# Expert lookups of a two-layer step: six units in one run, the part between the layers beside them, tile by tile

## The reference, cut to what matters

```python
ue = expert_u[idx]          # rows of 1024 floats, 128 for each token
ve = expert_v[idx]
act = jax.nn.gelu(jnp.einsum('td,thkd->thk', xb, ue).astype(f32))
coef = (gate * act).astype(xb.dtype)
return jnp.einsum('thk,thkd->td', coef, ve)
```

## Time and profile before

| | us |
|---|---|
| median of 3 runs | 3033.41 (3025.52 to 3058.54) |
| the profiled execution | 3040.26 |
| its span, first to last instruction | 3038.2 |
| VectorE busy | 1603.4 |
| TensorE busy | 1891.8 |
| GpSimd busy | 1523.8 |

### The profile page before, as it was taken

The page is one execution under the profiler, slowest core; times in us unless marked ns, Lnnn a source line. Parts: engine busy times, 40 slices in busy tenths (PEclk is TensorE's granted clock), DMA queues, the critical chain, the costliest instruction groups (busy, mean ns, idle before and its releaser), DMA issues. The chain is left out here.

```text
span 3038.2 us, 22434 instructions
## 1 busy us (share of the span) xinstructions
PE 1891.8 (62%) x7072; PEld 904.2 (30%) x7072; DVE 1603.4 (53%) x3822; ACT 284.2 (9%) x603; POOL 1523.8 (50%) x1480
## 2 busy tenths in 40 slices
PE   7999787890019900597767787790019900398547
PEld 4577564370002200122331356470002200122201
DVE  2488853148886079803734242248886078901731
ACT  2133210010000000000110133110000000000000
POOL 0013441017777777777645000017777777777672
PEclk9999887995559955798889867895559955699779
DMA  4332142248889999999888505238899999999896
GB/s 123 110 114 81 42 117 85 103 171 287 306 319 396 409 342 402 387 409 373 315 320 344 184 31 155 96 132 291 312 332 403 408 319 361 370 408 380 310 371 235
DMA packets 301933, 809.18 MB, mean 266 GB/s; under 512 B 26041, under 2 KB 91401, under 8 KB 301793
## 3 DMA queue, kind: packets, MB, share of 16 engines
q0 software_dynamic: 184320, 671.17, 58.5%
q1 hardware_dynamic: 117502, 136.65, 14.0%
HBM read 795.45 MB, written 12.17 MB: 266 GB/s over the span
## 5 line engine op out<-in xcount | busy, mean ns | idle before, releaser
L1919 POOL DMA_INDIRECT arena<-peer_u,arena x640 | 788.4, 1232 | 854.8 <-DVE arena L1599 563.7
L1620 DVE SCALAR_TENSOR_TENSOR arena<-arena,u 128x1024 f32<-128x1024 f32 x640 | 769.8, 1224 | 122.5 <-DMA arena<-peer_u,arena 105.2
L702 PE MATMUL banks<-arena 128*32 128x512 f32 x2560 | 782.2, 619 | 41.4 <-DMA arena<-peer_v,arena 34.8
L1919 POOL DMA_INDIRECT arena<-peer_v,arena x640 | 621.4, 971 | 251.4 <-issue 144.8
L476 PE MATMUL banks<-cst,arena 128*128 128x128 f32 (+5 forms) x522 | 85.7, 321 | 904.4 <-DVE arena L1635 661.3
L498 PE MATMUL banks<-wring,uT 128*128 128x512 f32 (+3 forms) x864 | 383.8, 601 | 12.1 <-DMA wring<-ssm_w_out 5.2
L702 PEld LDWEIGHTS banks<-arena 128*32 128x32 f32 x2560 | 200.1, 111 | 618.9 <-issue 335.5
L476 PEld LDWEIGHTS banks<-cst,arena 128*128 128x128 f32 (+5 forms) x522 | 68.9, 164 | 930.7 <-DVE arena L1635 664.7
L1662 DVE COPY h<-banks 128x512 f32<-128x512 f32 x8 | 5.5, 692 | 479.1 <-PE banks L709 479.1
L498 PEld LDWEIGHTS banks<-wring,uT 128*128 128x128 f32 (+1 forms) x864 | 150.1, 178 | 238.5 <-issue 233.8
L724 PE MATMUL banks<-uT,wring 128*128 128x320 f32 x512 | 140.7, 437 | 2.4 <-ACT uT L1073 2.4
(11 more groups left out here) (206 smaller groups left out, 1720.0 us busy)
## 6 DMA issues: line engine op xcount, KB each, us to landing
wring<-ssm_w_in SPq DMA_DIRECT2D x24, 1024.0 KB, 7.3
wring<-peer_w_query SPq DMA_DIRECT2D x16, 1024.0 KB, 7.4
wring<-ple_w_gate SPq DMA_DIRECT2D x16, 1024.0 KB, 5.8
wring<-w_q SPq DMA_DIRECT2D x12, 1024.0 KB, 8.6
arena<-peer_u,arena POOLq DMA_INDIRECT x640, 6.2
arena<-peer_v,arena POOLq DMA_INDIRECT x640, 7.2
wring<-ssm_w_out SPq DMA_DIRECT2D x8, 1024.0 KB, 7.3
u<-state_ssm SPq DMA_DIRECT2D x16, 512.0 KB, 6.1
```

The source lines that it names most:

```text
L702: mm = pe.matmul(outs[n][at % C], place(t)[:, at % C, at // C, :], rows_buf[:, k, n * 512:(n + 1) * 512], start=at < C, stop=False, skip_g ...
L1620: dve.scalar_tensor_tensor(rows_buf[:, k, :], rows_buf[:, k, :], 1.0, u[:, t, :], ALU.mult, ALU.mult, accum_out=cols[:, bass.ds(i, 1), k]) ...
L1919: pool.indirect_dma_start(rows_buf[:, k, :], None, tables[which], bass.IndirectOffsetOnAxis(ap=rows, axis=0))\
```

## The change

Seven phases follow each other in all engines' programs. Phase p has the u blocks of unit p and the v blocks of unit p-1, in the order of `phase_blocks`: 6 u, the v but 6, the remaining u, the last 6 v. Beside the blocks run side steps, spread evenly by `due`: the remaining selection of layer 0 in phases 0 and 1, the whole part between the layers with the selection of layer 1 for tile 0, 1 and 2 in phases 2, 3 and 4 (`chain(t)`), the embedding of layer 1 in phases 5 and 6, and after them that of tile 2. `chain(t)` is embedding, `kv`, `wq`, heads, attention of this tile alone (`prompt_attention` or `sample_attention`), `wo`, normalisation and `ask(t)`, the queries and picks of this tile.

All these weights are planned and loaded once per tile: the embeddings, `kv` and `wq` three times where it was twice, `wo` and the second queries three times where it was once. Queries of layer 1 are products of 128 or 64 columns where they had 320. Values are summed in banks 6 and 7, with the two halves of a block on different columns of the array for all tiles; the other jobs share six banks. The caches of the samples lie in the weight ring, singly buffered, so that no weights are loaded meanwhile. Dots are written out block by block instead of a loop. One quad is picked before the first gather; the other seven of tiles 0 and 1 lie beside the dots of tile 0.

```diff
-        def claim(pe, key, hold=False):
-            while turn[0] % NB in held:
...
+        def claim(pe, key):
+            b = turn[0] % ring[0]
...
+        UNITS = ((0, 0), (0, 1), (0, 2), (1, 0), (1, 1), (1, 2))
+        BLOCKS = (128, 128, 64)
+        LEAD = 6
+        def phase_blocks(ph):
+            nu = BLOCKS[UNITS[ph][1]] if ph < 6 else 0
+            nv = BLOCKS[UNITS[ph - 1][1]] if ph > 0 else 0
+            i = j = 0
+            while i < nu or j < nv:
+                if j == nv or (i < nu and (i < LEAD or j >= nv - LEAD)):
+                    yield "u", ph, i
+                    i += 1
+                else:
+                    yield "v", ph - 1, j
+                    j += 1
...
+        SIDE_STEPS = (39, 12, 51, 51, 48, 3, 3)
+        def due(ph, i):
+            upto = lambda k: SIDE_STEPS[ph] * k // PHASE_LEN[ph]
+            return upto(i + 1) - upto(i)
...
+            def sums(t, n, half):
+                if t == 2:
+                    at = 64 * half + COLS * (n % 2)
+                    return sum_banks[0][at:at + COLS, :]
+                at = COLS * ((n + 2 * half) % 4)
+                return sum_banks[half][at:at + COLS, :]
...
+            def beside(ph):
+                if ph == 0:
+                    yield from finish_select(0, 0, 5)
+                    yield from select(0, 1)
+                elif ph == 1:
+                    yield from select(0, 2)
+                elif ph < 5:
+                    yield from chain(ph - 2)
+                else:
+                    yield from embed(1, ph - 5)
...
+            for ph in range(7):
+                side = beside(ph)
+                for i, (kind, n, at) in enumerate(phase_blocks(ph)):
+                    if kind == "v":
+                        combine(n, at)
+                    advance(side, due(ph, i))
+                advance(side)
...
-        cache = arena[:, 15728:15728 + 4 * 3328].rearrange(
-            "p (x w b n) -> p x w b n", x=2, w=2, b=26)
+        cache = wring[:, :, :].rearrange("p s d -> p (s d)")[:, 0:2 * 3328].rearrange("p (w b n) -> p w b n", w=2, b=26)
...
-                with dve.Fori(first, last, 1) as i:
-                    for k in range(PSLOTS):
...
+            def dot(n, at):
+                (l, t), (k, use) = UNITS[n], turn_of["u", n, at]
+                dve.wait_ge(gathered[k].sem, 16 * (use + 1))
...
+            for ph in range(7):
+                for kind, n, at in phase_blocks(ph):
+                    (l, t), (k, use) = UNITS[n], turn_of[kind, n, at]
```

More of the change, by code:

```diff
@@ L715, in ffn, with turn_sub_keys, finish_select @@
[L715 removed]
+            def turn_sub_keys(l):
                 pe.wait_ge(*sk_in.at(l))
                 transposes(("sk", l), [(c * 128, sk_raw[:, c, :]) for c in range(2)])
[L718 to L720 removed]
+            def finish_select(l, t, first=0):
+                for _ in range(first, 5 * (HPT[t] // 2)):
+                    yield
+                turn_indices(l, t)
+                yield
@@ L721, in ffn, with select, ask, query @@
+            def select(l, t):
+                scores(l, t, range(HPT[t] // 2))
+                yield
+                yield from finish_select(l, t)
+            def ask(t):
+                R, cols = ROWS[t], slice(OFF[t], OFF[t] + ROWS[t])
+                def query(n):
+                    w = [weight(pe, (f"query1{t}", n, half), ("q1", t, 4 * n + 3)) for half in range(2)]
                     for j in range(4):
-                        acc = claim(pe, ("q", l, 4 * n + j))
+                        bank = claim(pe, ("q1", t, 4 * n + j))
@@ new lines, in ask @@
+                if t == 0:
+                    turn_sub_keys(1)
+                query(0)
+                yield
+                query(1)
+                if t == 0:
+                    pe.wait_ge(*freed(("sk", 1)))
+                if t < 2:
+                    turned(0)
+                    scores(1, t, [0])
+                yield
+                for q in range(4):
+                    if q < 2:
+                        query(q + 2)
+                    if t < 2 and q < 3:
+                        turned(q + 1)
+                        scores(1, t, [q + 1])
+                    if t == 2 and q == 1:
+                        for n in range(4):
+                            turned(n)
+                        scores(1, 2, range(2))
+                    if t < 2 or q < 2:
+                        for _ in range(5 if t < 2 else 1):
+                            yield
@@ L763, in embed @@
+                yield from finish_select(1, t, 20 if t < 2 else 0)
+            def embed(l, t):
+                R, cols = ROWS[t], slice(OFF[t], OFF[t] + ROWS[t])
+                pe.wait_ge(*prow_in.at((l, t)))
+                transposes(("pT", l, t), [(c * 128, p_rows[0:R, c * 128:(c + 1) * 128]) for c in range(2)])
+                norm_transposes(f"ple{l}", (t,))
+                pe.wait_ge(*freed(("pT", l, t)))
                 yield
                 for n in range(2):
-                    w = weight(pe, (f"pproj{l}{group}", n, 0), (f"pproj{l}", n, tiles[-1]))
@@ L1349, in _ @@
+            for ph in range(7):
+                side = beside(ph)
+                for i, (kind, n, at) in enumerate(phase_blocks(ph)):
+                    if kind == "u" and at + 1 == BLOCKS[UNITS[n][1]]:
+                        tanh_of(n)
+                    advance(side, due(ph, i))
+                advance(side)
+                if ph < 6:
+                    place_coefficients(ph)
+            advance(embed(1, 2))
         @block.vector
@@ new lines, in beside @@
+            def beside(ph):
+                if ph == 0:
+                    yield from finish_select(0, 0, 1)
+                    yield from select(0, 1)
+                elif ph == 1:
+                    yield from select(0, 2)
+                elif ph < 5:
+                    yield from chain(ph - 2)
+                else:
+                    yield from embed(1, ph - 5)
+            for n in range(2):
+                for t in range(3):
+                    add_to_h("out", 0, t, n)
+            norm("ffn0", FFN_SLOT)
@@ new lines, in _ @@
+            s(dve.tensor_copy(u[64:128, 2, :], u[0:64, 2, :]))
+            s(dve.memset(place, 0.0), dve_done, "place_zero")
+            advance(pick_quad(0, 0, 0))
+            for ph in range(7):
+                side = beside(ph)
+                for i, (kind, n, at) in enumerate(phase_blocks(ph)):
+                    if kind == "u":
+                        dot(n, at)
+                        if at + 1 == BLOCKS[UNITS[n][1]]:
+                            gelu(n)
+                    advance(side, due(ph, i))
+                advance(side)
+                if ph > 0:
+                    take_peer(*UNITS[ph - 1])
```

1193 lines of the change are left out of this document (588 added, 605 removed).

## The result

The changed kernel takes 3081.5 us (median of 4 runs, 3074.95 to 3084.61); the kernel before took 3040.55 us in the same comparison. The ratio is 1.0129 with an interval of 1.0067 to 1.0192: slower by 1.3%. The forecast was 2991 us and faster by 1.4%, so the change went the other way. The time lies within the stated range, nearest to rival C (3105 us).

The account below looks back on a forecast made before the run. No engine bounds the whole: DMA bounds value stages, VectorE is 85% busy in dot stages, 378 us lack gathers. Start, seven phases, handovers 18 and tail 46 sum to 2996 of span, so 2991 us; range 2840 to 3110.

Parts of the forecast that it names:

- rival C: Whole kernel: waits stall in-order engines, fronts cost 73 us in each of three tiles, slower at 3105 us; chance 0.22.
- Start, phases 0, 2, 3 and 5: Span before the first gather 663 us, then phases of 272, 387, 403 and 272 us.
- Tile 1's dot run: Phase 3: 140 + 28 + 62 of VectorE, then waits for scores and attention and light steps, 257 us.
- dot run: 140 + 19 + 31 + 20 of waiting + 15: Phase 4: VectorE's work, 20 us waiting for scores, 15 for steps with nothing in them, 225 us.
- the caches as 42 us of bytes: Phase 4's value run: 13.6 MB of cached keys and values at 321 GB/s, within a run of 250 us.
- a DMA share under 0.8 in value runs: Value runs: the sign that would show the slower rival, stalled in-order engines, to be right.
- its queries at the lower clock: Dot runs of phases 3 and 4: queries take twice as long, VectorE waits some 30 us more at the first quad.
- Rival D: Whole kernel: dots with gaps fall into the pace of 1.52 us, no change, 3025 us; chance 0.16.
- 1.39 us a dot block: Phase 1: pace taken for 128 dot blocks, after 128 value blocks at 1.31 us, 346 us in all.
- Phase 6 and the tail: End of the kernel: last phase 84 + 14 = 98 us, tail 46 us as before.
- The columns: Value blocks: halves on different column groups earn nothing by themselves but give side work 0.85 us a block.
- The rule on who interferes: Value runs: two-input VectorE instructions exclude GpSimd's SBUF reads, some 15 us a run by rule; trace has about nothing.

Follow-up runs that it names:

- run 17: Not a run label: the words belong to "the dot run 17 shorter", where phase 2's dot run was 17 us shorter than its terms.
- e13: Changed kernel with SyncE sending the cached keys of the next pair ahead of this pair's values: 3055.94 us, ratio 1.0063 to the kernel before.
- e2: Changed kernel with only the first sample pair's cached keys and values loaded, the other three pairs reusing them: 3027.65 us, ratio 0.9996 to the kernel before.
- e4: Changed kernel with two of the eight chunks of each layer 1 query product multiplied, weights loaded as before: 3061.48 us, ratio 1.011 to the kernel before.
- e6: Changed kernel with seven empty steps in phase 4's chain, so VectorE takes sample sums and tile 2's first quad later: 3069.98 us, ratio 1.0168.
- e8: Changed kernel with both halves of a value row of tiles 0 and 1 on the same group of 32 TensorE columns: 3094.99 us, ratio 1.0239.
- e5: Changed kernel with side steps weighted into the value runs, three to a value block and one to a dot block: 3109.99 us, ratio 1.0277.
- e11: Changed kernel with side steps weighted into the dot runs, one to a value block and three to a dot block: 3106.68 us, ratio 1.0241.
- e12: Changed kernel with a ring of six row slots instead of eight: 3147.95 us, ratio 1.0384 to the kernel before.
- e9: Changed kernel with three of tile 1's four quads picked in phase 1, mostly beside value blocks, instead of phase 0: 3053.12 us, ratio 1.0065.

## Why the prediction was wrong

- **Start, phases 0, 2, 3 and 5: within 14 us, in part by errors that cancel.** Phase 0 took 258 us: VectorE was busy for 245 (I had 258) and idle for 13 (I had 14). In phase 2 the value run was 10 us longer and the dot run 17 shorter than its terms. Tile 1's dot run took 240 us against 257: VectorE's work was 208 us where I had 230, the waiting 28 where I had 22, of which 11.2 for attention and 8.7 for the scores (I had 8 and 14). VectorE's waits there:

```profile
DVE arena L1850 <- PE banks L774: 11.2, 2, 8.3
DVE arena L1681 <- ACT arena L1250: 8.7, 1, 8.7
```

- **The step that failed: phase 4, "dot run: 140 + 19 + 31 + 20 of waiting + 15", and the caches as 42 us of bytes.** Of the 66 us, 51 are the dot run (276 against 225) and 17 the value run (267 against 250); the edges give 2 back. The work in the dot run (190 us) was right and the waiting mis-sized: 92 us instead of 35. The wait for scores was as priced (23.8 against 20). What had no price was the sample pairs: I put three of the four into the value run and gave the rest no wait, and the third and fourth cost 27.7 + 11.3 + 3.3 us there, and 25.5 us went to late rows. And I took the cache's single buffer as bytes: the loads of one pair wait for the products of the one before, and the keys stood behind the values in SyncE's queue. With the keys ahead (e13) the value run is at 251 us, against my 250, and phase 4 is 26 us shorter with the same bytes; without the three later caches (e2) it is 55 shorter.
- **The dot run of phase 4 is VectorE's work plus its waits.** Its length less the sum of VectorE's waits is 183 to 186 us in the changed kernel and in e2, e4, e6, e8 and e13, while the waits sum to 92, 71, 73, 56, 88 and 81 us. So a wait removed there shortens the run. But the waits replace each other in part: without the wait for scores (e4) the dots waited 6 us more for rows, with later consumers (e6) 19 us more, and there the value run grew by 22; moving steps either way (e5, e11) made phase 4 longer.
- **Rival C was the nearest, and half right.** Its mechanism is there: chains cut by tile cost 300 us more than joined, and the ring drains when an engine is away (e12). But its sign, a DMA share under 0.8 in value runs, did not appear (0.93 and 0.90 in those of phases 2 and 4), and its queries at the lower clock showed in phase 4 alone: those of tile 1, in the dot run of phase 3, have a median of 275 ns like tile 0's. Three quarters of all queries' products are worth 21 us of span (e4).
- **Rival D was real, in phase 1.** I took 1.39 us a dot block and it was 1.56 in phase 1: +19 us. Its sign, 1.35 us for a mean issue of u, was not reached (1.296). Why this run falls into the slow pace and the stage at 1060 before did not, no run shows. Phase 6 and the tail added 12 and 11; the cause of these is open.
- **The columns: right that they earn little.** But my reason, 0.85 us a block of room for the side work, was hardly needed (e8).
- **The rule on who interferes: it holds, and its price was nothing.** Beside the dots, which read two SBUF operands, an issue goes from 0.94 to 1.97 us (the timeline below). Beside picks it lengthens too. The value run of phase 1 in e9, GpSimd and then VectorE:

```profile
941.00 0.94 POOL L2056 DMA_INDIRECT arena<-peer_v,arena  x1 [0.30 <-issue]
942.25 1.35 POOL L2056 DMA_INDIRECT arena<-peer_v,arena  x1 [0.30 <-issue]
...
942.09 0.69 DVE L1722 TENSOR_TENSOR arena<-arena 128x512 f32<-128x512 f32 x1
```

The page "SBUF — State Buffer" of the Trainium skill ("Who interferes with whom") says that a VectorE instruction with two SBUF inputs contends with a GpSimd instruction that reads SBUF. The trace agrees: in that run, from 915 us on, every issue that met no such instruction took 0.93 to 0.95 us, and those that met one took up to 1.35. But six issues above 1.0 us among over a hundred cost nothing, since a value run goes at the DMA's pace of 1.31 us a block and an issue with its 0.30 us takes 1.24: the run was as long (158 us) with 62 us of picks beside it as with 30. The prediction's rows were right about the cost, not about the contention.

What stays open: how the 40 us of phase 4 that remain with the keys ahead (534 against 494) divide between clock, late rows and late scores; the runs show that they move into one another. A deeper ring was not tried, since the arena as it is laid out has no room for it.

## What to carry to other kernels

Before cutting a batched part into pieces to hide it, price the pieces alone: here 451 us became 758, and hiding 328 of them only broke even, so that a loss of 51 us elsewhere (picks put beside dots, and a dot run at the slow pace) set the sign. A chain of small steps over in-order engines did not hide by its bytes or its busy time alone, so look for the wait that stalls the stream (a load behind another in a queue, a copy that stands ahead of the urgent instruction, a single buffer) before moving work about. And mix two kinds of blocks that different engines consume, rather than run them one after the other: that was worth 2.1% here with the same steps. With six slots instead of eight the mixed order lost 3.8% and the order of runs 2.5%, so the mix needs its ring.

## What the hardware showed that I had not expected

An issue of GpSimd beside dots varies between 0.93 and 1.99 us from one to the next. The timeline of GpSimd in the dot run of phase 1:

```profile
1138.99 1.97 POOL L2052 DMA_INDIRECT arena<-peer_u,arena  x1 [0.31 <-issue]
1141.26 0.94 POOL L2052 DMA_INDIRECT arena<-peer_u,arena  x1 [0.30 <-issue]
1142.51 0.93 POOL L2052 DMA_INDIRECT arena<-peer_u,arena  x1 [0.30 <-issue]
```

In phase 4 issues settled near 1.7 us, with a dot every 2.04, for 20 to 30 us at a time (2425 to 2453, 2483 to 2503). SyncE was held for 10.43 us by one piece of a cache (L1086), about as long as the eight slots last. A matmul of 64 columns at the lower clock takes 421 ns, one of 128 columns at the higher 275.
